# VectorE's order in the convolution stage, and dense products in three passes, in a hybrid decoder kernel

## The reference

```python
x = layer_norm(ALPHA * x + 0.5 * swiglu(x, ffn1_w_gate, ffn1_w_up, ffn1_w_down), ln1_g, ln1_b)
proj = x @ w_in
c_q, c_kv, k_rope, xbar, b_gate, c_gate, u_s5, gates = jnp.split(proj, ...)
y_a = mla_branch(c_q, c_kv, k_rope, ...)      # attention from low-rank latents, 8 heads
y_b = short_conv_branch(xbar, b_gate, c_gate, ...)  # (b_gate * causal_conv3(c_gate * xbar)) @ w_out
y_c = s5_branch(u_s5, ...)                    # state-space branch, GELU, gate, projection
g = jax.nn.sigmoid(gates.reshape(B, L, N_BRANCH, D_MODEL))
mixed = g[:, :, 0] * y_a + g[:, :, 1] * y_b + g[:, :, 2] * y_c
x = layer_norm(ALPHA * x + mixed @ w_o, ln2_g, ln2_b)
x = layer_norm(ALPHA * x + 0.5 * swiglu(x, ffn2_w_gate, ffn2_w_up, ffn2_w_down), ln3_g, ln3_b)
```

## Time and profile before

| | |
|---|---|
| median of 3 runs | 2890.27 us (2888.03 to 2891.69) |
| profiled execution | 2893.35 us, of which its span 2890.6 us |
| TensorE busy | 94% of the span |
| VectorE, ScalarE, GpSimd busy | 48%, 29%, 37% |
| mean granted TensorE clock | 0.972 of full |

### The profile page before, as it was taken

The page is one execution under the profiler, slowest core; times in us unless marked ns, Lnnn a source line. Parts: engine busy times, 40 slices in busy tenths (PEclk is TensorE's granted clock), DMA queues, the critical chain, the costliest instruction groups (busy, mean ns, idle before and its releaser), DMA issues.

```text
span 2890.6 us, 56692 instructions
## 1 busy us (share of the span) xinstructions
PE 2710.9 (94%) x22244; PEld 2628.9 (91%) x22244; DVE 1396.7 (48%) x2020; ACT 845.8 (29%) x1236; POOL 1058.6 (37%) x477
## 2 busy tenths in 40 slices
PE   7999998899999989999889999798999999999996
PEld 7999988888889989999789999798888998999995
DVE  6954154935443662121688641649344436522126
ACT  3222223135532242222242222232245222422223
POOL 4444433312234434444334444233222343344431
PEclk9999999999999999999999999899999999999998
DMA  4323323212223323232223232232122232233322
GB/s 142 95 81 92 88 76 81 70 28 59 57 70 87 99 66 92 86 92 84 70 86 88 87 93 84 64 89 63 41 52 60 73 94 88 74 93 88 88 80 73
DMA packets 458206, 229.27 MB, mean 79 GB/s; under 512 B 38112, under 2 KB 455136, under 8 KB 458048
## 3 DMA queue, kind: packets, MB, share of 16 engines
q1 hardware_dynamic: 452864, 219.98, 27.3%
q10 hardware_dynamic: 5184, 7.14, 0.9%
HBM read 222.83 MB, written 2.10 MB: 78 GB/s over the span
## 4 chain that ended last, share of the span: by engine, by line
issue 51%; PE 25%; POOL 21%; DVE 2%; POOLq 1%; ACT 0%; DMA 0%; SPq 0%; DVEq 0%; ACTq 0%
POOL w_lo L393 21%; PE ps L438 21%; PE ps L454 1%; PE ps L737 1%; PE ps L699 1%; PE ps L716 0%; DVE ln_in L1128 0%; POOLq L392 0%; PE ps L703 0%; DVE stat L1143 0%; PE ps L463 0%; DVE stat L1159 0%; DVE ln_in L1112 0%; DVE stat L1129 0%; POOLq L398 0%
## 5 line engine op out<-in xcount | busy, mean ns | idle before, releaser
L393 POOL TENSOR_TENSOR w_lo<-w_raw,w_hi 128x1024 fp32r<-128x1024 f32 (+3 forms) x472 | 1055.9, 2242 | 1785.5 <-ACT w_hi L825 1785.3
L438 PE MATMUL ps<-x_hi,w_hi 128*128 128x264 f32 x4000 | 827.8, 288 | 20.0 <-DVE ln_in L1193 10.2
L438 PE MATMUL ps<-x_lo,w_hi 128*128 128x264 f32 x4000 | 817.6, 286 | 0.0
L438 PE MATMUL ps<-x_hi,w_lo 128*128 128x264 f32 x4000 | 816.8, 286 | 0.0
L825 ACT ACTIVATE w_hi<-w_raw 128x1024 fp32r<-128x1024 f32 (+3 forms) x475 | 453.8, 959 | 867.3 <-PE ps L438 736.9
L438 PEld LDWEIGHTS ps<-x_hi,w_hi 128*128 128x128 f32 x4000 | 627.1, 189 | 32.3 <-issue 24.3
L438 PEld LDWEIGHTS ps<-x_lo,w_hi 128*128 128x128 f32 x4000 | 622.3, 189 | 0.0
L438 PEld LDWEIGHTS ps<-x_hi,w_lo 128*128 128x128 f32 x4000 | 621.6, 189 | 0.0
L1180 DVE TENSOR_TENSOR hid_rest<-hid_rest,ps 128x528 f32<-128x528 f32 x88 | 61.9, 704 | 564.3 <-PE ps L438 537.4
L438 PE MATMUL ps<-hid_hi,w_hi 128*128 128x264 f32 x1408 | 292.5, 289 | 13.4 <-DVE ln_in L1112 12.5
L438 PE MATMUL ps<-hid_lo,w_hi 128*128 128x264 f32 x1408 | 289.6, 287 | 0.0
(11 more groups left out here) (272 smaller groups left out, 3134.4 us busy)
## 6 DMA issues: line engine op xcount, KB each, us to landing
w_raw<-in_ffn_w_gate SPq DMA_DIRECT2D x91, 512.0 KB, 3.8
w_raw<-in_w_in SPq DMA_DIRECT2D x90, 512.0 KB, 3.9
w_raw<-in_ffn_w_up SPq DMA_DIRECT2D x88, 512.0 KB, 3.8
w_raw<-in_ffn_w_down SPq DMA_DIRECT2D x64, 512.0 KB, 3.9
w_raw<-in_ffn_w_down SPq DMA_DIRECT2D x32, 384.0 KB, 3.4
w_raw<-in_w_o SPq DMA_DIRECT2D x16, 512.0 KB, 3.9
w_raw<-in_conv_w_out SPq DMA_DIRECT2D x16, 256.0 KB, 2.8
w_raw<-in_s_w_out SPq DMA_DIRECT2D x16, 256.0 KB, 3.2
```

The costliest lines, as they stand in the source:

```text
L393: pool.tensor_tensor(w_lo[:, s, 0:n], w_raw[:, c % RAW, 0:n], w_hi[:, s, 0:n].bitcast(f32), ALU.subtract).then_inc(w_split, 1)
L438: ins = nc.tensor.matmul(out[0:m, h], w[:, s, cols], x[:, k0 + k, h * HALF:(h + 1) * HALF], start=first and k == 0 and n == 0, stop=last a ...
```

## The change

Two edits. First, VectorE does convolution tile 2 directly after tile 1, then `latents_begin`, then tile 3, and both sets of latent tiles behind it.

Second, `product` runs over all tiles of the chunk with `w_hi` and `x_hi`, then over all with `w_hi` and `x_lo`, then over all with `w_lo` and `x_hi`. In most of the dense products TensorE waits at the start only for the rounded weights (`rounded`), and for the split ahead of the third pass. Products of the heads, `glu`, `w_o`, and chunk `bu + 3` of a feed-forward block keep the whole wait at the start and change only their order; `first_products` is as it was. The down product that reads the hidden tiles in two pieces waits for both at the start.

```diff
+            def rounded(l, c, it_chunks=0):
+                pe.wait_ge(w_rounded, l * CH + it_chunks + (c + 1))
+
-            def product(out, c, k0, hi, lo, n_tiles, first, last, m=P, at=0):
+            def product(out, c, k0, hi, lo, n_tiles, first, last, m=P, at=0, split=None):
 
                 s = c % SLOTS
-                for k in range(n_tiles):
-                    cols = slice((at + k) * m, (at + k + 1) * m)
-                    parts = ((w_hi, hi), (w_hi, lo), (w_lo, hi))
-                    for n, (w, x) in enumerate(parts):
+                for n, (w, x) in enumerate(((w_hi, hi), (w_hi, lo), (w_lo, hi))):
+                    if n == 2 and split is not None:
+                        split_ready(*split)
+                    for k in range(n_tiles):
+                        cols = slice((at + k) * m, (at + k + 1) * m)
                         for h in range(2):
                             ins = nc.tensor.matmul(out[0:m, h], w[:, s, cols], x[:, k0 + k, h * HALF:(h + 1) * HALF],
                                                    start=first and k == 0 and n == 0,
                                                    stop=last and k == n_tiles - 1 and n == 2)
...
-                            split_ready(l, c, i * 4)
+                            rounded(l, c, i * 4)
                             pe.wait_ge(silu_done, n0 + i * 2 + (j + 1))
-                            product(pair(2 * j), c, 0, xh, xl, KD, True, True).then_inc(chunk_done, 1)
-                            split_ready(l, c + 1, i * 4)
+                            product(pair(2 * j), c, 0, xh, xl, KD, True, True, split=(l, c, i * 4)).then_inc(chunk_done, 1)
+                            rounded(l, c + 1, i * 4)
...
                     def down(d, at_loop, hid):
                         c = bd + d
-                        split_ready(l, c, at_loop)
+                        rounded(l, c, at_loop)
                         pe.wait_ge(z_taken, t0 + at_loop + (d + 1))
                         if hid:
+                            split_ready(l, c, at_loop)
...
                         else:
-                            product(pair(d % 2), c, 0, gh, gl, nf, True, True).then_inc(chunk_done, 1)
+                            product(pair(d % 2), c, 0, gh, gl, nf, True, True, split=(l, c, at_loop)).then_inc(chunk_done, 1)
...
                 conv_tile(l, 1, st)
+                conv_tile(l, 2, st)
                 latents_begin(l, st)
+                conv_tile(l, 3, st)
                 latent_tiles(l, 0, st)
-                conv_tile(l, 2, st)
                 latent_tiles(l, 1, st)
-                conv_tile(l, 3, st)
                 s5_outputs(l, st)
```

More of the change, by code:

```diff
@@ L495, in ffn @@
                             c = bu + 2 * j
-                            split_ready(l, c, i * 4)
+                            rounded(l, c, i * 4)
                             pe.wait_ge(silu_done, n0 + i * 2 + (j + 1))
-                            product(pair(2 * j), c, 0, xh, xl, KD, True, True).then_inc(chunk_done, 1)
-                            split_ready(l, c + 1, i * 4)
+                            product(pair(2 * j), c, 0, xh, xl, KD, True, True, split=(l, c, i * 4)).then_inc(chunk_done, 1)
+                            rounded(l, c + 1, i * 4)
                             pe.wait_ge(hid_done, n0 + i * 2 + (j + 1))
-                            product(pair(2 * j + 1), c + 1, 0, xh, xl, KD, True, True).then_inc(chunk_done, 1)
+                            product(pair(2 * j + 1), c + 1, 0, xh, xl, KD, True, True, split=(l, c + 1, i * 4)).then_inc(chunk_done, 1)
                     pe.wait_ge(silu_done, n0 + (nf + 1))
@@ L553, in m1 @@
                         s5_states_in(l)
-                    split_ready(l, c)
+                    rounded(l, c)
                     pe.wait_ge(m1_taken, l * (N_M1 - 1) + min(n + 1, STATES_AT))
@@ L557, in m1 @@
                         pe.wait_ge(f_taken, l * MT + (n - STATES_AT + 1))
-                    product(pair(n % 4), c, 0, xh, xl, KD, True, True).then_inc(chunk_done, 1)
+                    product(pair(n % 4), c, 0, xh, xl, KD, True, True, split=(l, c)).then_inc(chunk_done, 1)
             def s5_states_in(l):
@@ L595, in conv @@
                         s5_toeplitz(l)
-                    product(pair(CONV_PAIR[n]), c, 0, xh, xl, KD, True, True).then_inc(chunk_done, 1)
+                    product(pair(CONV_PAIR[n]), c, 0, xh, xl, KD, True, True, split=(l, c)).then_inc(chunk_done, 1)
             def s5_toeplitz(l):
@@ L786, in merge @@
                             c = B_MERGE + 2 * n
-                            split_ready(l, c, i * 8)
+                            rounded(l, c, i * 8)
                             pe.wait_ge(gate_sig, l * 2 * KD + i * 4 + (n + 1))
-                            product(pair(2 * (n % 2)), c, 0, xh, xl, KD, True, True).then_inc(chunk_done, 1)
-                            split_ready(l, c + 1, i * 8)
+                            product(pair(2 * (n % 2)), c, 0, xh, xl, KD, True, True, split=(l, c, i * 8)).then_inc(chunk_done, 1)
+                            rounded(l, c + 1, i * 8)
                             pe.wait_ge(merge_mul, l * 2 * KD + i * 4 + (n + 1))
@@ L793, in merge @@
                                 pe.wait_ge((s_split, o_split)[r], l * MT + MT)
-                            product(pair(2 * (n % 2) + 1), c + 1, 0, yhi, ylo, MT, True, True).then_inc(chunk_done, 1)
+                            product(pair(2 * (n % 2) + 1), c + 1, 0, yhi, ylo, MT, True, True, split=(l, c + 1, i * 8)).then_inc(chunk_done, 1)
             def w_o(l):
```

## The result

The changed kernel takes 2849.18 us at the median, the kernel before 2890.98 beside it; the ratio is 0.9855, 95% interval 0.9838 to 0.9872. The direction and the first term were right; a second term, of about the same size, had been set to nothing.

The account below looks back on a forecast made before the run. TensorE, busy 94% of the span, was taken as the bound. Per layer 8.3 + 1.8 - 0.3 = 9.8 us, 19.6 over two, and 0 for the pass order, gave 2870.7 us; 8-in-10 range 2861 to 2881.

Parts of the forecast that it names:

- the first term: VectorE's new order in the convolution stage: 9.8 us less per layer, 19.6 us over two layers.
- a second term: Dense products pass by pass: the new matmul order was taken to change the time by 0.
- The gap at the Toeplitz matmuls: TensorE's wait before `s5_toeplitz` for VectorE to take chunk 7 would vanish: 8.3 us less per layer.
- The clock term: Toeplitz matmuls, 5.81 us, would run at clock 1.00 once the wait is gone: 1.8 us less per layer.
- The new wait of 0.3 us: At TensorE's third S5 tile, the first S5 output taken too late behind five latent tiles: 0.3 us per layer.
- No hold by GpSimd: Latents behind tile 3 fall where GpSimd is idle, so no split holds VectorE; otherwise at most 4.8 us over both layers.
- Rival B: Latents behind tile 3 come late, by a split's hold or longer tiles: up to 2.4 us per layer, 2875.5; chance 0.10.
- The deferred wait, gain 0: Dense products starting before their `w_lo` is there gain 0, as no affected product showed a wait for the split.
- Its cost, taken as 0: One more wait inside each of 340 products costs 0; 41 us if each hand-over of 0.12 us shows.
- rival D: The mid-product wait for the split is paid on TensorE: 2912 at 0.12 us a product; chance 0.06.
- The distance between matmuls, taken as 0, with 11 us kept to both sides: In dense products, new order leaves the matmul interval unchanged; a 0.7 ns shift over 16,224 matmuls would be 11 us.
- rival C: Pass order moves the matmul interval by 0.7 ns: 2860 or 2882; chance 0.07 down, 0.06 up.

Follow-up runs that it names:

- e3_wait_first: Changed kernel with the whole wait for the split back at the start of every product; 2851.00 us, ratio 0.9868 to the kernel before.
- e2_pass_order: Kernel before with only the matmul order in `product` changed to three passes, VectorE's order and split wait as before; 2870.92 us, ratio 0.9927.
- a1: Kernel before with VectorE's new order, products in old order, `x_lo` and all behind it moved 128 bytes; 2854.73 us, ratio 0.9878.
- f1: Kernel before with VectorE's new order, products in old order, `w_lo` and all behind it moved 128 bytes; 2867.02 us, ratio 0.9938.
- a2: Kernel before with VectorE's new order, products in old order, tiles of `x_hi` and `x_lo` 2304 bytes apart; 2849.83 us, ratio 0.9863.
- m1: Changed kernel, split waited for at the start, two passes: per tile `w_hi` then `w_lo` with `x_hi`, then all `w_hi` with `x_lo`; 2860.41 us.
- m2: Changed kernel, split waited for at the start, two passes: per tile `w_hi` with `x_hi` then `x_lo`, then all `w_lo` with `x_hi`; 2858.44 us.
- m3: Changed kernel with three passes, each taking the tiles in the order 0, 4, 1, 5, 2, 6, 3, 7; 2866.09 us, ratio 0.9918.
- f2: Kernel before with VectorE's new order, products in old order, tiles of `x_hi` and `x_lo` 2176 bytes apart; 2879.66 us, ratio 0.9974.

## Why the prediction was wrong

**The gap at the Toeplitz matmuls**: right. The waits of 8.3 us are gone. The clock term of 1.8 us a layer measured 5.81 - 3.66 = 2.15 in layer 0 and 2.02 in layer 1: the whole 5.81 us scaled with the clock (times 0.63 it is 3.66), and the part held back for time between the groups did not show. The new wait of 0.3 us did not come, by a hair: the take of the first S5 output ended 12.4 us after chunk 11 and not 12.6, 0.06 us ahead of the tile that needs it. Forecast 19.6 us, measured alone 21.5 (by the interval of its ratio 16 to 26).

**No hold by GpSimd**: right. The latents took 9.8 us for five tiles, none longer than normal. Rival B did not come.

**The deferred wait, gain 0**: right within what `e3_wait_first` can tell. **Its cost, taken as 0**: the same; rival D did not come.

**The distance between matmuls, taken as 0, with 11 us kept to both sides**: this is the step that failed, and it failed twice. The size: the only measure I had, 0.7 ns between two layers with one code, was taken as the most that an order could do, and the change was 1.4 to 1.6 ns, twice that. On all 18,624 matmuls of `product` 1.4 ns is 26 us; `e2_pass_order` measured 18.0 us (by its interval 16 to 27). The choice: rival C had this case on one side, with 0.07, because nothing in the trace tied the distance to the order of operands. Its rows did hold a warning. Two layers with the same code, the same addresses and the same clock ran at 121.7 and 122.4 ns, so the distance was no fixed property of the instruction and 0 was not a safe value for it. But these were two steady values of the old order, and neither said what another order would do. With the 18.0 us measured, the forecast of 2870.7 becomes 2852.7; the kernel took 2849.18.

What the runs put in its place: with the order unchanged, 128 bytes ahead of `x_lo` or of `w_lo`, or tiles of x spaced by 2304 bytes, change the distance (a1, f1, a2); orders with the same sequence of starts modulo 256 bytes are alike place by place (m1, m2, and m3's second pass). That the addresses of both operands count is shown, and for the moving operand that 256 bytes is the step. They do not decide alone: equal code on equal addresses has more than one steady distance, and what picks one is open. What in the chip makes it so is not shown either: reading of the two operands against each other is a guess that no run here separates, and why 2176 bytes is worse than 2112 and the three passes better than the old order stays open.

## What to carry to other kernels

When one engine is bound by a stream of equal instructions, measure their distance from start to start before and after any reordering or change of layout; a single nanosecond on 18,000 matmuls is as much as the best gap in this kernel. Measure it in several stretches of a trace, since one code can settle at different values after different pauses. In the products whose operand had a pitch of a multiple of 256 bytes the order of the matmuls stopped mattering and the distance was the shortest seen, but another padding cost as much as it gave, so each is to be measured. And a wait that precedes no idle time in the list of waits is worth nothing to defer.

## What the runs showed of the hardware

The distance between two matmuls of 264 columns at the full granted clock was not one number: by order and layout its mean lay between 120.0 and 122.9 ns, and the means by place between 115.8 and 128.4 ns. At each place these means were alike to 0.1 ns in `m1_weights_switch` and `m2_moving_switch`. The addresses of both operands modulo 256 bytes enter (a1, a2, f1, f2), and so does the history: the old order ran whole rows of products at 121.7 ns and others at 122.3. 264 columns at 2.4 GHz are 110 ns.

The Trainium skill (TensorE: Matmul & The Clock Gate, section "Wait — 56ns, not 53.3ns?") gives the distance of back-to-back matmuls as the columns over the clock and about 2.5 ns more; for 264 columns that is an estimate of 112.5 ns. By that rule no order and no padding would have changed the time. The traces differ from it by 7.5 to 10.4 ns, and that difference depends on order and layout; each of these matmuls has a weight load of its own (22,244 of each). For such pairs another section of the page ("Back-to-back issue gap") gives about 81 ns at 128 columns and 131 at 512; 264 columns at 120 ns and more lie well above a line between the two (about 99 ns, an estimate from that page), so neither figure sizes these matmuls, and the measurement decides.
